# Modulations at other places, the normaliser written in the odd layer, the combination's products in one block, and the first experts' loads in another order

## What is computed

```python
def trunk_layer(x, mod, P, l, ctx):
    sh1, sc1, g1, sh2, sc2, g2 = jnp.split(mod, 6, axis=-1)      # mod = silu(c) @ ada_w[l] + ada_b[l]
    h = rms_norm(x, P['norm_mix'][l]) * (1 + sc1) + sh1
    if l % 2 == 0:
        out, st = even_mixer(h, P, l // 2, ctx)
    else:
        out, st = odd_mixer(h, P, l // 2, ctx)
    x = x + g1 * out
    h = rms_norm(x, P['norm_ffn'][l]) * (1 + sc2) + sh2
    x = x + g2 * hier_moe(h, P, l)
```

## Time and profile before

| | us |
|---|---|
| runs of before, median (lowest to highest) | 1378.31 (1373.08 to 1378.74) |
| profiled execution, own time | 1375.63 |
| its span | 1373.3 |
| TensorE busy | 1217.6 (89%) |
| VectorE busy | 508.8 (37%) |
| ScalarE busy | 367.3 (27%) |
| GpSimd busy | 116.2 (8%) |
| bytes read from and written to HBM | 320.04 MB and 29.53 MB |

### The profile page before, as it was taken

The page is one execution under the profiler, slowest core; times in us unless marked ns, Lnnn a source line. Parts: engine busy times, 40 slices in busy tenths (PEclk is TensorE's granted clock), DMA queues, the critical chain, the costliest instruction groups (busy, mean ns, idle before and its releaser), DMA issues. The chain is left out here.

```text
span 1373.3 us, 16060 instructions
## 1 busy us (share of the span) xinstructions
PE 1217.6 (89%) x5914; PEld 710.7 (52%) x5914; DVE 508.8 (37%) x1066; ACT 367.3 (27%) x756; POOL 116.2 (8%) x142
## 2 busy tenths in 40 slices
PE   5999967888998999788899999999989989988883
PEld 3555634334884333233456555889879733333333
DVE  3005453334243111011364884778852611110014
ACT  2102504335231111111234433553542221111111
POOL 1500010000001111111000000200000111111100
PEclk9999978989999999999999999999989899999997
DMA  9962478168549999998533120010152899999971
GB/s 363 325 247 83 178 210 305 63 245 307 215 160 389 416 418 415 404 416 354 201 93 123 62 93 0 1 32 1 62 193 84 339 404 415 408 418 403 404 289 46
DMA packets 87921, 329.04 MB, mean 240 GB/s; under 512 B 19183, under 2 KB 25497, under 8 KB 66976
## 3 DMA queue, kind: packets, MB, share of 16 engines
q1 hardware_dynamic: 72560, 297.40, 56.0%
q0 software_dynamic: 15280, 30.56, 6.5%
HBM read 320.04 MB, written 29.53 MB: 255 GB/s over the span
## 5 line engine op out<-in xcount | busy, mean ns | idle before, releaser
L992 PE MATMUL psum<-wide,ring 128*128 128x384 f32 x704 | 241.7, 504 | 3.8 <-ACT wide L1709 1.9
L992 PEld LDWEIGHTS psum<-wide,ring 128*128 128x128 f32 x704 | 165.5, 238 | 72.0 <-issue 7.9
L1364 PE MATMUL psum<-arena 128*64 128x512 f32 x568 | 157.3, 607 | 14.8 <-DMA arena<-in_moe_w_up 9.6
L992 PE MATMUL psum<-ring,wide 128*128 128x512 f32 (+2 forms) x336 | 118.7, 511 | 0.0
L2443 DVE TENSOR_TENSOR arena<-arena,psum 128x256 f32<-128x256 f32 x34 | 14.3, 421 | 272.2 <-ACT arena L1863 272.2
L1364 PEld LDWEIGHTS psum<-arena 128*64 128x64 f32 x568 | 51.0, 139 | 115.2 <-issue 115.1
L1863 ACT ACTIVATE arena<-psum 128x256 f32<-128x256 f32 x34 | 13.1, 384 | 305.6 <-PE psum L1364 305.6
L1364 PE MATMUL psum<-ring,arena 128*64 128x512 f32 x320 | 76.5, 634 | 12.6 <-DMA ring<-in_moe_w_up 12.6
L992 PEld LDWEIGHTS psum<-ring,wide 128*128 128x128 f32 x336 | 58.9, 195 | 53.4 <-issue 52.6
L1018 PE MATMUL psum<-ring,sil 128*32 128x512 f32 x368 | 61.3, 799 | 26.5 <-DMA ring<-in_ada_w 24.7
L1364 PE MATMUL psum<-wide,arena 128*64 128x512 f32 x160 | 73.9, 617 | 0.0
(11 more groups left out here) (528 smaller groups left out, 1740.9 us busy)
## 6 DMA issues: line engine op xcount, KB each, us to landing
ring<-in_ada_w SPq DMA_DIRECT2D x23, 2048.0 KB, 13.1
arena<-in_moe_w_gate SPq DMA_DIRECT2D x24, 1024.0 KB, 12.1
arena<-in_moe_w_up SPq DMA_DIRECT2D x24, 1024.0 KB, 20.2
arena<-in_moe_w_down SPq DMA_DIRECT2D x24, 1024.0 KB, 23.2
ring<-in_moe_w_gate SPq DMA_DIRECT2D x20, 1024.0 KB, 15.5
ring<-in_moe_w_up SPq DMA_DIRECT2D x20, 1024.0 KB, 20.7
ring<-in_moe_w_down SPq DMA_DIRECT2D x20, 1024.0 KB, 22.3
ring<-in_w_in_odd SPq DMA_DIRECT2D x7, 2048.0 KB, 9.1
```

The costliest lines, as they stand in the source:

```text
L992: ins = mm(out, lhs(k), rhs(k), start=(k == 0), stop=(k == n - 1))
L1364: ins = mm(psum[half, 2 + s, :].rearrange("p (w f) -> p w f", w=2), hg[s][:, k, half], gate_up_of(UNITS[q][h], k), start=(k == 0), stop=(k ...
```

## The change

It has four parts.

- The ten modulations beside other work get other places: five stay (N1 0, 2, 4, cqT, hmT); the other six are before the fourth q product, before "qR", before "vv", and at attention steps (0,0), (1,0) and (1,4).
- VectorE copies the normalisers into eight spare columns of `colsT`, and GpSimd writes them to DRAM after the gate gain of the odd layer. `even_out` counts 80 at the waits inside the layers, 112 only at the end.
- In the combination the eight products with `hot_last` are issued in one block, then the wait for `chosen_added`, then the transposes of all eight banks.
- In `moe` on SP: after unit 0, still ahead of the wait for "o", come the gate and up parts of the patched expert and of one expert of unit 1; behind it gate and up of the other and both down parts; then a wait for the transposes "hr" and the gate part of the expert in `wide`, before the waits of before. Buffer 3 has its gate and up part in ring slot 2 and its down part in the second half of slot 1.

```diff
@@ -168,8 +168,8 @@
 
 def mods_beside():
 
-    places = [("N1", 2 * pair, 0) for pair in range(3)] + [("cqT", 0), ("hmT", 0)]
-    places += [("pT", c, h) for c, h in ((0, 1), (0, 6), (1, 2), (1, 6), (2, 2), (2, 6))]
+    places = [("N1", 2 * pair, 0) for pair in range(3)] + [("cqT", 0), ("hmT", 0), ("qf", 3), ("qR", 0), ("vv", 0)]
+    places += [("pT", c, h) for c, h in ((0, 0), (1, 0), (1, 4))]
     parts = MOD_PARTS[MODS_FIRST:]
     assert len(places) == len(parts) + 1
 
@@ -383,6 +383,7 @@
         amp = sb("amp", [P, 2, 2, KD, 2])
         rows = sb("rows", [P, P])
         colsT = sb("colsT", [P, P])
+        n_out = colsT[:, 120:128].rearrange("p (d h) -> p d h", d=2)
         wr = sb("wr", [P, 2, KD, ROUTES])
         br = sb("br", [P, 2, ROUTES])
         route = sb("route", [P, 12, TILES, ROUTES])
@@ -434,6 +435,8 @@
 
         one = gate_up_words + down_words
         buffers = [(gu[n], dn[n]) for n in range(2)] + [expert_buffer(ring_words[:, n * one:(n + 1) * one]) for n in range(2)]
+        buffers[3] = (ring[:, 2, :].rearrange("p (w k f) -> p w k f", w=2, k=KD),
+                      ring[:, 1, down_words:].rearrange("p (j d) -> p j d", j=2))
         buffers += [None, expert_buffer(wide[:])]
         last_columns = (mod_rows[:], cst[:, C_COS:C_COS + 2 * FF])
         patch_down = (gain_row[:, 0:D], route[:].rearrange("p a c n -> p (a c n)")[:, 0:D])
@@ -667,11 +670,11 @@
 
             kind_ = "gathered_"
 
-            def gate_up_in(l, n, e):
+            def gate_up_in(l, n, e, which=(0, 1)):
                 if n >= BUFFERS:
                     sp.wait_ge(S(f"{kind_}gu_computed"), PAIRS * l + UNIT_OF[n - BUFFERS] + 1)
                 arrived = S(f"{kind_}gu{n % BUFFERS}_in")
-                for w in range(2):
+                for w in which:
                     src = expert_weights(l)[w][bass.ds(e, 1)].rearrange("e (p k) f -> p (e k) f", k=KD)
                     if n % BUFFERS != PATCHED:
                         sp.dma_start(buffers[n % BUFFERS][0][:, w], src).then_inc(arrived, 16)
@@ -736,7 +739,7 @@
                         sp.dma_start(shift_dram[l][j].rearrange("k p -> p k"), modT[:, l, 3, :, j]).then_inc(S("shift_out"), 16)
                 if l == 0:
                     sp.wait_ge(*taken("pv", TILES - 1, MLA_H // 2 - 1))
-                    sp.wait_ge(S("even_out"), 112)
+                    sp.wait_ge(S("even_out"), 80)
                 else:
                     sp.wait_ge(*computed("mT", 7))
                     sp.wait_ge(S("odd_out"), 64)
@@ -745,13 +748,19 @@
                     sp.dma_start(shift_rows[j], shift_dram[l][j].rearrange("k p -> (k p)").partition_broadcast(P))\
                         .then_inc(S("shift_in"), 16)
                 load_unit(l, 0)
-                sp.wait_ge(*computed("o", l, KD - 1))
-                load_unit(l, 1)
                 patched, in_wide = UNITS[2]
                 gate_up_in(l, patched, fixed(patched))
+                sooner, later = UNITS[1][::-1] if l == 0 else UNITS[1]
+                gate_up_in(l, sooner, fixed(sooner))
+                sp.wait_ge(*computed("o", l, KD - 1))
+                gate_up_in(l, later, fixed(later))
+                for n in UNITS[1]:
+                    down_in(l, n, fixed(n))
+                sp.wait_ge(*computed("hr", l, TILES - 1, 1))
+                gate_up_in(l, in_wide, fixed(in_wide), (0,))
                 sp.wait_ge(S("h_rows_out"), 16 * TILES * (l + 1))
                 sp.wait_ge(*computed("h0", l, 1))
-                gate_up_in(l, in_wide, fixed(in_wide))
+                gate_up_in(l, in_wide, fixed(in_wide), (1,))
                 down_in(l, in_wide, fixed(in_wide))
                 sp.wait_ge(S("expert_ids"), 3 * l + 3)
                 down_in(l, patched, fixed(patched))
@@ -887,7 +896,6 @@
                 for d in range(2):
                     pool.dma_start(o["C"][0, 0, d].rearrange("h k v -> k h v"),
                                    mlC[:, 0, d, :, 0:P]).then_inc(S("even_out"), 16)
-                    pool.dma_start(o["n"][0, 0, d].rearrange("h k -> k h"), mlC[:, 0, d, :, P]).then_inc(S("even_out"), 16)
                 pool.dma_start(o["m"][0, 0].rearrange("d h -> (d h)").unsqueeze(0),
                                mst[0:1, 0, :, :].rearrange("p d h -> p (d h)")).then_inc(S("even_out"), 16)
 
@@ -919,6 +927,8 @@
                 pool.wait_ge(*taken("zg", TILES - 1))
                 gate = zg.rearrange("p c (h n) -> p (c h) n", h=4)
                 nc.gpsimd.tensor_tensor(gate, gate, bc(ggdn, 1, [P, 12, P]), ALU.mult).then_inc(S("gate_gain"), 1)
+                for d in range(2):
+                    pool.dma_start(o["n"][0, 0, d].rearrange("h k -> k h"), n_out[:, d]).then_inc(S("even_out"), 16)
                 for d in range(2):
                     pool.wait_ge(*taken("SU", d))
                     pool.dma_start(o["gdn"][0, 0, d].rearrange("h k v -> k h v"),
@@ -1176,10 +1186,12 @@
                 ready(ins)
 
             for h in range(MLA_H):
+                beside("qf", h)
                 b = issue("qf", h)
                 pe.wait_ge(*taken("cqT", 2))
                 ready(contract(b[0:QK_DIM, 0:T], lambda k: w_uq[:, k, h * QK_DIM:(h + 1) * QK_DIM],
                                lambda k: cqT[:, k, :], 3))
+            beside("qR", 0)
             for i in range(4):
                 b = issue("qR", i)
                 pe.wait_ge(*taken("qf", 2 * i + 1))
...
@@ -1454,17 +1467,17 @@
                 slot_lists(l)
                 gathered(l)
 
+                pe.wait_ge(S("hot_last"), l + 1)
                 for m in range(KD):
                     b = issue("yt", l, m)
-                    if m == 0:
-                        pe.wait_ge(S("hot_last"), l + 1)
                     mm(b[:, 0:T], yrow[(PAIRS - 1) % 2][:, m::KD], hot_last, start=True, stop=False)
-                    if m == 0:
-                        pe.wait_ge(S("chosen_added"), TILES * (l + 1))
+                pe.wait_ge(S("chosen_added"), TILES * (l + 1))
+                for m in range(KD):
+                    b = bank("yt", l, m)
                     for c in range(TILES):
                         ins = mm(b[:, tok(c)], ysel[0][:, c, m::KD], ident, start=False, stop=(c == TILES - 1),
                                  is_transpose=True)
-                    ready(ins)
+                    ready(ins, "yt", l, m)
 
             shift_products(0)
             for m in range(4):
@@ -1767,20 +1780,23 @@
                 act.wait_ge(*computed("kvT", k))
                 take(fn(kvT[:, k, :], bank("kvT", k), ACT.Copy), "kvT", k)
             beside("hmT", 0)
-            act.wait_ge(S("even_out"), 112)
+            act.wait_ge(S("even_out"), 80)
             for h in range(4):
                 act.wait_ge(*computed("hmT", h))
                 take(fn(mix[:, h, :], bank("hmT", h)[:, 0:T], ACT.Copy), "hmT", h)
-            act.wait_ge(S("even_out"), 112)
+            act.wait_ge(S("even_out"), 80)
             act.wait_ge(S("k_rot"), 1)
             fn(kfT[NOPE:QK_DIM, :, :], bc(kpe[NOPE:QK_DIM, :], 1, [ROPE, MLA_H, KEYS]), ACT.Copy).then_inc(S("keys"), 1)
             for h in range(MLA_H):
+                beside("qf", h)
                 act.wait_ge(*computed("qf", h))
                 take(fn(qfT[0:QK_DIM, h, :], bank("qf", h)[0:QK_DIM, 0:T], ACT.Copy), "qf", h)
+            beside("qR", 0)
             for i in range(MLA_H // 2):
                 act.wait_ge(*computed("kn", i))
                 fn(kfT[0:NOPE, 2 * i, :], bank("kn", i)[0:NOPE, :], ACT.Copy)
                 take(fn(kfT[0:NOPE, 2 * i + 1, :], bank("kn", i)[NOPE:2 * NOPE, :], ACT.Copy), "kn", i)
+            beside("vv", 0)
             scale = QK_DIM ** -0.5
 
             def exponentials(n):
@@ -2227,6 +2243,8 @@
                                      "CU", u, half)
                             else:
                                 take(v.tensor_copy(mlC[:, 0, d, both], two_of(bank("CU", u, half))), "CU", u, half)
+                        if not sequence:
+                            o_(v.tensor_copy(n_out[:, d], mlC[:, 0, d, :, P]))
 
 
             dve.wait_ge(S("roots"), 2)
@@ -2246,6 +2264,9 @@
             take(tt(rtmp[r, 0:SAMPLE], sinT[r], bank("kpR")[r, 0:SAMPLE], ALU.mult), "kpR")
             o_(tt(kpe[r, 2 * P:4 * P], kpe[r, 2 * P:4 * P], cosT[r], ALU.mult))
             done(tt(kpe[r, 2 * P:4 * P], kpe[r, 2 * P:4 * P], rtmp[r, 0:SAMPLE], ALU.add), "k_rot")
+            for h in range(MLA_H):
+                beside("qf", h)
+            beside("qR", 0)
             for i in range(4):
                 q = qfT[r, 2 * i:2 * i + 2, PROMPT:T]
                 dve.wait_ge(*computed("qR", i))
...
```

More of the change, by code:

```diff
@@ L2496, in before_experts @@
                 if l == 0:
-                    dve.wait_ge(S("even_out"), 112)
+                    dve.wait_ge(S("even_out"), 80)
                     dve.wait_ge(*taken("pv", TILES - 1, MLA_H // 2 - 1))
```

## The result

| | before | after |
|---|---|---|
| median of the runs, us (lowest to highest) | 1376.49 (1373.08 to 1378.74) | 1343.18 (1341.93 to 1347.11) |
| ratio, 95% interval | | 0.9764 (0.9738 to 0.9791) |
| profiled execution, its span | 1375.63, 1373.3 | 1341.93, 1339.6 |
| TensorE busy, mean granted clock | 1217.6, 0.947 | 1203.1, 0.960 |

The changed kernel is 33 us faster, 2.4%. A second comparison, beside the last experiments, gave 1344.03 against 1373.63, ratio 0.9780 (0.9745 to 0.9815). The forecast was 1349, with a range from 1340 to 1362. Two launches of the first experiments, 1452 us with part 1 alone and 1804 of before, ran at a mean granted clock of 0.83 and 0.65 and are left out of the ratios.

What follows compares the result with a forecast made beforehand. TensorE, busy 89% of 1373.3 us, plus its waits bounds the kernel. Terms -9.5 - 13.5 - 8.6 + 1.7 = -29.9 take 1375.6 to 1345.7, in terms of the median 1348.4; forecast 1349, range 1340 to 1362.

Steps and rivals of the forecast that it cites:

- Part 1: Scans, even layer: without the normaliser writes, modulation 2's weights land near 191, not 198.8; 9.5 us gained, bounds 0 to 10.2.
- the row of the very stretch: Profile row from 182 to 186 us: DMA engines 92% busy moving 27 GB/s; reason to take 9.5 us, near the upper end.
- Part 2: Attention and q to v stages: modulations 5 to 9 moved ahead run without DMA waits; 13.5 us gained, bounds 6 to 15.1.
- The discount of 1.6 for a falling clock: Attention: 13.5 us taken instead of up to 15.1, as the clock may fall between thin products.
- Part 3: First experts: less in the DMA stream after the row writes, and an earlier restart; 4.3 us a layer, 8.6 in all.
- the gate part at its full 2.5 us: First experts: the wide buffer's gate part, 1.05 MB, leaves the full DMA stream; 2.5 us.
- the restart: First experts: row writes land sooner and the stream restarts at 419.8; up to 2.9 us in layer 0, 2 in layer 1.
- rival (c): Experts: the stream runs dry before 438.6 and gives back its gain, leaving 0 to 3 us; 1356 us, chance 0.12.
- TensorE's waits for expert weights: Experts: sign expected of the load reordering; these waits shrink by some 4 us a layer.
- Part 4: Combination: blocked products start no earlier, only the order changes; layer 0 taken as 0, layer 1 1.7 us slower.
- the scaling behind the additions: Combination: VectorE scales the last output row's second half after three additions; TensorE waits for that, until 669.3 in layer 0.

Runs made afterwards that it cites:

- part 1 alone: The kernel before, with only the normaliser writes moved from the even to the odd layer; 1363.01 us against 1375.46, ratio 0.9919.
- part 3 alone: The kernel before, with only the order of the first experts' loads changed; 1368.56 us against 1375.46, ratio 0.9950.
- part 4 alone: The kernel before, with only the combination's eight products issued in one block ahead of the wait; 1373.43 us against 1375.46, ratio 1.0001.
- the two row writes: The changed kernel plus two 2 KB writes at the old even-layer place, each 4 rows of 512 bytes, from a constant; 1336.31 us, ratio 0.9702.
- parts 2, 3 or 4 alone: Three kernels, each the one before with only moved modulations, reordered expert loads or blocked combination products; 1359.72, 1368.56 and 1373.43 us against 1375.46.

## Why the prediction held, point by point

**Part 1** (forecast 9.5 by choice, 10.2 by its own working; measured 10.3 at "hmT"). Each step came as worked out: start "about 191" (191.10), 3.85 us at full clock (3.81), the gain passed on to modulations 3 and 4. Taking the row of the very stretch over the general rule was right. The Trainium skill ("DMA: Bandwidth & Descriptors", Why small descriptors are slow) names about 3 cycles of fixed overhead for a packet and its metadata, and by that alone this gain would have been nearly 0. These traces don't agree where elements of 4 bytes are written: 4 KB of them cost the modulations behind 10 us. The part was worth more than the sum had, by 3 us at the very end of the span (below).

**Part 2** (forecast 13.5; the working on the time line gave 15.1; measured 14.9 and, alone, 16.5 from "hmT" to the end of attention). The path is right: no wait for weights but 0.4 us, 3.8 us for each modulation, and the two steps in 3.31 us of the earlier trace rows. The discount of 1.6 for a falling clock looks too careful in this profile, where the clock fell from 284 to 290, cost 0.7 us on each of three wide score products, and was up again for modulation 9. In four of the ten kernels with part 2 it was not up again:

```profile
291.45 6.01 PE L1028 MATMUL psum<-ring,sil 128*32 128x512 f32 x32
```

That is the kernel with the scaling first, where the stretch took 102.7 us. The mean of the ten is 100.0, that of the four without part 2 113.4: 13.4 us, the forecast with its discount.

**Between the parts** one term was not in the sum. The first output product of layer 0 runs at full clock in every kernel with part 2 (5.53 us, without it 6.2 to 8.0), a gain of 1.3. The two other differences here are not the change's. The router's products of layer 0 ran at 0.50 from 387 to 391 (8.40 us instead of 7.16), but so they did with part 3 alone (8.37). And the first output product of layer 1, 5.52 instead of 7.91, takes one or the other time with and without the change (5.53 with part 4 alone, 8.03 with the two row writes). The odd layer, from the sum of squares to its last shift product, took 330.5 us instead of 328.3. That is no work of the n writes there: over the other kernels with part 1 this stage took between 326.7 and 330.6 us, and with part 4 alone 330.5.

**Part 3** (forecast 4.3 a layer; measured 4.2 and 2.5, in the second profile of the change 3.4 and 1.1, alone 4.5 and 3.6). It was sized too high, in layer 1 above all: its lower bound was 2.5. The step that gave 4.3 was to take the gate part at its full 2.5 us and to add 1.8 of at most 2.9 for the restart; the middle of its bounds, 2.5 and 5.4, would have been 4.0. That the emptier queue would run dry stood there as rival (c), and it does: 0.3 to 0.4 of 1.05 MB are missing in the first 10 us. Nor did TensorE's waits for expert weights shrink, as was said they would; what shrank is the wait for gathered rows, by 3.7 us over both layers, and the slow first 20 us of the stage in layer 0 (TensorE is busy for 17.6 of them instead of 15.9).

**Part 4** (forecast 0 and +1.7; alone, no difference). No earlier start, as said. From the start of the combination to the sum of squares it takes 10.2 us instead of 11.3 in layer 0, which is 1.1 better than forecast; to the fourth square in layer 1 it takes 15.4 instead of 13.1, 2.2 worse, where 1.7 was forecast. The mechanism named for it, the scaling behind the additions, is shown by the two kernels that put it first.

The sum of the parts was 29.9, and at the fourth square of the final norm the gain is 30.7: the errors, +0.8 in part 1, +1.4 in part 2, -1.9 in part 3, +0.6 in part 4 and 0.0 between the parts, partly cancel. What the sum missed is the last 3.0 us. Another 1.8 of the 6 us by which 1349 is too high lie in its start: it was reckoned from 1378.3, the median of three runs of before, which with the fourth is 1376.5. The mechanisms of parts 1, 2 and 4 held, each with its number. That the total of stages comes within 1 us of the sum is in part luck: single profiles of the stages differ by more, and the two comparisons of the change differ in their gain by 3.7 us (33.3 and 29.6).

## What to carry to other kernels

Where the DMA engines show busy and move next to nothing, look for a write in single elements, and move it to where no load is behind it, or give it rows. When an edit puts work ahead of a wait, look at what the engine on the other side does first: reordering TensorE brought nothing until VectorE's scaling went ahead of its additions, and from then on it was worth 7 us. A load moved out of a full stream pays only while the stream stays full behind it (half the up part ahead changed nothing), so look for a hole in the first stretches of the stage. And before a stage's gain of 1 or 2 us is explained, compare two profiles of the same kernel.

## What the hardware showed that was not expected

The end of the span is shorter with part 1. The last output write is issued at 1363.02 in before and 1332.30 in after, and lands 2.9 us later in both, but the span ends 10.3 us behind the issue in before and 7.3 in after:

```profile
1332.30 0.53 POOL L945 DMA_DIRECT2D out_ys<-wide  x1 [1.73 <-DVE wide L2782]
```

It is so in every kernel: 10.3 us in before and with parts 2, 3 or 4 alone, 7.2 to 7.3 in all ten others, which have part 1 (1351.48 to 1358.7 with it alone). The profile shows no instruction and no DMA in the last microseconds (from 1366 in before and 1336 in after), and the extra writes of 2 KB in rows don't bring the 3 us back. Part 1 as a whole makes the difference. Whether it is the time of the writes, 180 or 842 us, or their source, which part 1 changes too, stays open.

Two writes of 2 KB in elements of 4 bytes hold up far larger transfers, of their own queue (kv 15.0 us instead of 2.9, C 5.5 instead of 3.1) and of SyncE's (a weight load of 2 MB landing at 198.8 instead of by 191.1).

A short standstill of TensorE costs twice: after 3.7 to 6.6 us of waiting the block of the combination took 7.1 to 8.1 us (ten cases in five kernels), after 0.90 us 5.53 (six cases in three).
